# A mixture-of-experts stage on one TensorE: weights stationary and tokens streaming in the gate and up products

## The reference, cut to what matters

```python
    # top-1 of 4 groups, top-2 of 8 experts in it: 2 slots per token, sorted by expert,
    # each expert's slots padded to blocks of MOE_BLOCK = 128
    xs = h_pad[slot_tok].reshape(n_blocks, MOE_BLOCK, d)

    def expert_block(args):
        xb, e = args
        return (jax.nn.silu(xb @ exp_w_gate[e]) * (xb @ exp_w_up[e])) @ exp_w_down[e]

    yb = lax.map(expert_block, (xs, blk_e)).reshape(n_slots, d)
```

## Time and profile before

| | |
|---|---|
| median of 3 runs | 8363.2 us (8362.91 to 8382.72) |
| the profiled execution | 8377.1 us, span 8375.4 us |
| mean granted TensorE clock | 0.877 |
| PE busy | 6258.6 us (75%) |
| PEld busy | 4170.1 us (50%) |
| DVE busy | 4465.4 us (53%) |
| ACT busy | 3932.8 us (47%) |
| POOL busy | 1101.7 us (13%) |
| DMA | 751.33 MB, mean 90 GB/s |

### The profile page before, as it was taken

The page is one execution under the profiler, slowest core; times in us unless marked ns, Lnnn a source line. Parts: engine busy times, 40 slices in busy tenths (PEclk is TensorE's granted clock), DMA queues, the critical chain, the costliest instruction groups (busy, mean ns, idle before and its releaser), DMA issues. The chain is left out here.

```text
span 8375.4 us, 113418 instructions
## 1 busy us (share of the span) xinstructions
PE 6258.6 (75%) x38615; PEld 4170.1 (50%) x38615; DVE 4465.4 (53%) x10927; ACT 3932.8 (47%) x7814; POOL 1101.7 (13%) x1560
## 2 busy tenths in 40 slices
PE   6999976888777877888888771632299969999950
PEld 2777752555455555555555450621155546677630
DVE  0221227878778778888877749246255631010025
ACT  0212215788777878888888750123232312222124
POOL 1222210000000000000000000022022223333333
PEclk8999988999999999999999985765588879999975
DMA  5211210000000000000000001225432238888877
GB/s 191 63 59 59 61 55 3 8 11 11 10 11 11 11 11 11 10 9 10 10 11 9 6 23 45 101 72 61 64 96 94 90 131 327 325 336 335 321 270 246
DMA packets 315242, 751.33 MB, mean 90 GB/s; under 512 B 110701, under 2 KB 174189, under 8 KB 272568
## 3 DMA queue, kind: packets, MB, share of 16 engines
q0 software_dynamic: 70400, 424.79, 13.8%
q1 hardware_dynamic: 244388, 321.14, 13.0%
q10 hardware_dynamic: 54, 0.30, 0.0%
HBM read 582.03 MB, written 162.11 MB: 89 GB/s over the span
## 5 line engine op out<-in xcount | busy, mean ns | idle before, releaser
L955 PE MATMUL at_pC<-at_mark,at_identb 128*128 128x256 bf16 (+1 forms) x5708 | 756.7, 283 | 385.9 <-DVE at_mark L1090 303.8
L1012 DVE CUSTOM_DVE_ANT_0 at_sm<-at_pS,at_drop 128x512 f32<-128x512 f32 (+3 forms) x1152 | 696.1, 642 | 321.1 <-PE at_pS L911 319.1
L955 PEld LDWEIGHTS at_pC<-at_mark,at_identb 128*128 128x128 bf16 x5708 | 531.3, 101 | 638.8 <-DVE at_mark L1090 463.8
L846 ACT ACTIVATE at_sm<-at_sm,at_negm 128x512 f32<-128x512 f32 (+3 forms) x1152 | 785.6, 695 | 58.7 <-DVE at_negm L1017 58.3
L911 PE MATMUL at_pS<-keep_KT,at_q 64*128 64x512 f32 (+3 forms) x2304 | 648.1, 641 | 204.8 <-DVE at_mx L1012 204.5
L1004 DVE SCALAR_TENSOR_TENSOR at_score<-at_relu,keep_IW,at_score 128x512 f32<-128x512 f32 (+3 forms) x994 | 660.2, 706 | 120.5 <-ACT at_relu L831 116.9
L901 PE MATMUL at_pD<-keep_IKT,at_iq_stack 128*128 128x512 bf16 (+3 forms) x2272 | 579.5, 377 | 147.6 <-ACT at_relu L831 97.5
L932 PEld LDWEIGHTS at_pO<-at_pt_sb,keep_V 128*64 128x64 f32 x8448 | 470.6, 141 | 416.4 <-issue 291.1
L831 ACT ACTIVATE at_relu<-at_pD 128x512 f32<-128x512 f32 (+3 forms) x1136 | 580.7, 568 | 105.9 <-PE at_pD L901 66.5
L921 PE MATMUL at_pT<-keep_ident,at_sm 128*128 128x128 f32 x4224 | 588.6, 282 | 40.6 <-DVE at_out L1026 32.5
L932 PE MATMUL at_pO<-at_pt_sb,keep_V 128*64 128x128 f32 x8448 | 613.3, 288 | 0.1
(11 more groups left out here) (442 smaller groups left out, 10892.3 us busy)
## 6 DMA issues: line engine op xcount, KB each, us to landing
scratch_ys<-ex_y SPq DMA_DIRECT2D x96, 512.0 KB, 2.6
ada_w_sb<-in_ada_w SPq DMA_DIRECT2D x12, 2048.0 KB, 8.0
scratch_x<-mx_x SPq DMA_DIRECT2D x33, 512.0 KB, 7.5
scratch_h<-mx_h SPq DMA_DIRECT2D x33, 512.0 KB, 2.6
cb_x<-scratch_x SPq DMA_DIRECT2D x33, 512.0 KB, 4.4
pj_x<-in_x_prompt SPq DMA_DIRECT2D x32, 512.0 KB, 3.6
mx_x<-in_x_prompt SPq DMA_DIRECT2D x32, 512.0 KB
out_y_prompt<-cb_out SPq DMA_DIRECT2D x32, 512.0 KB, 3.6
```

What stands on the lines that cost most here:

```text
L846: last = e.activation(row, row, ACT.Exp, bias=negm[:, x.group % 16, kv:kv + 1], scale=-1.0, accum_out=den[:, x.side, kv * G + x.g, x.c:x.c ...
L955: last = e.matmul(pC[:, side, 0:b - a], identb[:, :], mark[:, a:b], start=a == at.start, stop=not constant and b == at.stop)
L1012: last = e.tensor_tensor_reduce(sm[:, u % RING, kv, 0:x.width], pS[:, kv, 0:x.width], drop[:, o:o + x.width], -HD ** -0.5, -NEG, ALU.add, ...
```

## The change

Gate and up products change sides: a block of 128 x 128 of the weights is stationary and the 128 tokens of xT stream past it. The results then come out with the inner width on the partitions, in two pieces of 128 columns, and g is at once what the down products take. The transposes of g, the tile pH, VectorE's copy and the semaphores g and gT go; hT gets two buffers; VectorE's second product is written to hT, after a wait for the down products of two blocks before; TensorE's gate product waits for hT of the block before in place of g.

```diff
-        sg = sb("ex_sg", [P, FE]); gu = sb("ex_gu", [P, FE]); g = sb("ex_g", [P, FE]); hT = sb("ex_hT", [P, FC, P]); y = sb("ex_y", [P, 2, D])
-        pT = pb("ex_pT", [P, DC, P]); pg = pb("ex_pg", [P, CUT]); pu = pb("ex_pu", [P, CUT]); pH = pb("ex_pH", [P, FC, P]); pY = pb("ex_pY", [P, 2, CUT])
+        sg = sb("ex_sg", [P, FE]); gu = sb("ex_gu", [P, FE]); hT = sb("ex_hT", [P, 2, FC, P]); y = sb("ex_y", [P, 2, D])
+        pT = pb("ex_pT", [P, DC, P]); pg = pb("ex_pg", [P, CUT]); pu = pb("ex_pu", [P, CUT]); pY = pb("ex_pY", [P, 2, CUT])
...
                         pair(e, "w", b, par, 2)
-                        wait(e, s["g"], b)
+                        wait(e, s["hT"], b)
                         for dst, src in ((pg, wg), (pu, wu)):
-                            for c in range(DC):
-                                last = e.matmul(dst[:, 0:FE], xT[:, par, c, :], src[:, par, c * FE:(c + 1) * FE], start=c == 0, stop=c == DC - 1)
+                            for f in range(FC):
+                                for c in range(DC):
+                                    block = src[:, par, c * FE:(c + 1) * FE].rearrange("p (f c) -> p c f", c=FC)[:, f, :]
+                                    last = e.matmul(dst[:, f * P:(f + 1) * P], block, xT[:, par, c, :], start=c == 0, stop=c == DC - 1)
                         last.then_inc(s["gu"], 1)
...
-                                last = e.matmul(pY[:, k, :], hT[:, c, :], wd[:, q, c * D + k * CUT:c * D + (k + 1) * CUT], start=c == 0, stop=c == FC - 1)
+                                last = e.matmul(pY[:, k, :], hT[:, q, c, :], wd[:, q, c * D + k * CUT:c * D + (k + 1) * CUT], start=c == 0, stop=c == FC - 1)
                             last.then_inc(s["down"], 1)
-                    b = st
-                    if valid(b):
-                        e.wait_ge(s["g"], b + 1)
-                        wait(e, s["hT"], b)
-                        gv = g[:, :].rearrange("p (f c) -> p c f", c=FC)
-                        for c in range(FC):
-                            last = e.transpose(pH[:, c, :], gv[:, c, :], ident)
-                        last.then_inc(s["gT"], 1)
...
-                        wait(e, s["gT"], b)
                         e.tensor_tensor(gu[:, :], pg[:, 0:FE], sg[:, :], ALU.mult).then_inc(s["gsig"], 1)
                         e.wait_ge(s["gsig"], b + 1)
-                        e.tensor_tensor(g[:, :], pu[:, 0:FE], gu[:, :], ALU.mult).then_inc(s["g"], 1)
-                        e.wait_ge(s["gT"], b + 1)
-                        wait(e, s["down"], 2 * b)
-                        e.tensor_copy(hT[:, :, :], pH[:, :, :]).then_inc(s["hT"], 1)
+                        wait(e, s["down"], 2 * (b - 1))
+                        e.tensor_tensor(hT[:, par, :, :].rearrange("p c n -> p (c n)"), pu[:, 0:FE], gu[:, :], ALU.mult).then_inc(s["hT"], 1)
+                        e.wait_ge(s["hT"], b + 1)
```

## The result

| | before | after |
|---|---|---|
| median | 8389.2 us (15 runs, 8362.9 to 8394.6) | 8405.7 us (15 runs, 8390.4 to 8418.3) |
| ratio | | 1.0025, 95% interval 1.0016 to 1.0033 |
| the profiled execution | 8377.1 us, clock 0.877 | 8390.4 us, clock 0.879 |

The change costs 0.25%: +21 us, between +13 and +28 (the two medians lie 16.5 us apart, which is within that). Forecast was +6 with -1 to +14. With more runs than stood ahead of the prediction the median of before is 8389, so absolute times say less than the ratio. One thing is to be known about the profile of after: it shows the fastest of its 15 executions (8390.4; the clock averaged over all 15 is 0.877, not 0.879).

The account below looks back on a forecast made before the run. The weights' loop through POOL and DMA was taken to bound most steps: 0.23 us growth x 0.31 is 0.07, times 96 +7 us, ends -0.95, together +6 on 8363.2, giving 8369 us; range 8348 to 8400.

Parts of the forecast that it names:

- the size of a pass: Gate and up in the experts: 64 passes over 128 columns at 111.7 ns each, 7.15 us, growing by 0.23 us.
- the upper bound of 0.31: Largest growth in us of gate and up per step, at 113 ns per pass as in the transposes of x.
- The base of the absolute time: Median of the runs before, 8363.2 us, to which the forecast added +6 us to give 8369 us.
- less 1 for the end: Last down products no longer wait for the transposes of g and the copy: -0.95 us, once.
- The share of 0.31: Part of a growth in the weights' loop through POOL and DMA that reaches the step period, a/(1+a).
- a slope of -0.45: Line through 64 steps: a wd issued 1 us later moves the weights two steps on by only 0.45 us.
- The slot of the transposes and VectorE's copy: Removed 0.22 us of TensorE and 0.42 us of VectorE per step, outside the loop; TensorE's counts only in 17 steps without wait.
- the rival of a held POOL: VectorE's copy of hT delays POOL's wd; removal gains up to 12 us, about 8350; chance 0.11, shared with fewer clock drops.
- The first rival: Longer waits ahead of the gate product make TensorE's clock drop more often: +34 us to about +80; chance 0.10.
- Loads that are not hidden: Rival: gate and up's 0.19 us weight loads surface under 108 ns streams; +190 to about +390 us; chance 0.04.
- the serial case: Gate and up's loads fully serial: 64 x 0.19 is 12.2 us, step 16.8 us, about +390 us, 8760.
- Same: Outcome that whole-kernel time stays within 25 us (0.3%), what a measurement can tell; chance 0.78.

Follow-up runs that it names:

- e2_proj_stride2: Kernel before with the projection's stationary blocks at line 496 taken as every second column of 256, not 128 contiguous ones; 128 passes take 15.09 us, time 8411 us.
- e3_keep_slot: Changed kernel, but TensorE still does two transposes of hT, into a tile nobody reads, behind the down products; ratio 1.0020 to before.
- the filled pair: Kernel before and changed kernel, each with three useless products (0.67 us) ahead of each wait for gate weights; ratios 0.9979 and 1.0018 to before.
- e4: Kernel before without the transposes of g and VectorE's copy, second product written untransposed to hT, gate and up products unchanged; ratio 1.0008 to before.
- e1: Changed kernel with gate and up's stationary blocks as 128 contiguous columns instead of every second column; ratio 1.0024 to before.
- e11: Kernel before with wd fetched one step later, behind the next block's wg and wu, with its own index tile; 8276.4 us, ratio 0.9852 to before.

## Why the prediction was wrong, point by point

**The step that failed is the size of a pass.** The prediction took 111.7 ns from line 496 "for it is the same operation", and from the transposes of x that a stride adds next to nothing. It is not the same operation: with every second column as the stationary side it takes 117.8 ns, in the experts and in the projection alike. Gate and up grew by 0.63 us, not by 0.23, twice the upper bound of 0.31. The transposes of x, with a stride of eight, do run at some 112 ns, and why that stride costs them next to nothing was not found. That they are transposes is not the reason, for the trace of before holds the very stride of two as well, in the transposes of g (line 2233), whose loads the prediction did not use:

```profile
L2233 PEld LDWEIGHTS ex_pH<-keep_ident,ex_g x192: 194/196/222, 6862.7 to 8074.1; 128*128 128x128 f32 x192
```

Their median is the 196 ns of e2_proj_stride2, where the earlier trace rows have 193 for the stride of eight. And the second transpose of g starts 118 ns ahead of the first of x, on the average, against 109 in e3_keep_slot, whose two transposes take contiguous columns of hT. A neighbouring row bounded the price of one difference through another stride, and that was no bound.

**The base of the absolute time.** Of the 42.5 us between the 8363.2 that the forecast started from and the 8405.7 measured, 26 are the base: two of the three executions that it had were the two fastest of the fifteen. On 8389.2 the forecast's +6 would have been 8395. This is bad luck and a range too narrow for three runs; it says nothing of the mechanism, while the +0.25% against the forecast's +0.07% does.

**The working behind it fits, but its share is not shown.** With the measured 0.63 the prediction's own formula gives 0.63 x 0.31 x 96 = 19 us, less 1 for the end: +18, inside the measured +13 to +28. This is one sum against one number. The share of 0.31 comes from a slope of -0.45, and that depends on which steps are kept: by the gate starts of the same stretch it is -0.46 for the 65 steps that have a wait under 1.9 us and no slow gate in them or next, -0.11 with those next to a slow gate, and -0.26 if waits under 0.3 us are left out instead. The share that reaches the period should be more than 0.31 in the steps that have no wait, where TensorE's own work counts in full (+0.41 us); the filled pair, with most steps of that kind, fits: 33 us, of 39 possible.

**The slot of the transposes and VectorE's copy: right.** Outside the loop, worth nothing on balance (e3, e4). In e4 the wd gather starts 11.42 us after the gate, as with the copy, so the rival of a held POOL falls; in after it is 12.05 us, later by the 0.63 us, where 11.65 was forecast.

**The clock: the mechanism was seen, its direction was not.** The first rival said that the change lengthens waits and so brings clock drops, and by 0.06 us only. In fact TensorE's work grew by 0.41 us per step and the profiled run of after has fewer slow gates (3, though over all runs its mean clock equals that of before). What the prediction lacked is that more waiting and more slow gates come with shorter work as well. Two cases fit: e1 (0.39 us less for the passes, no gain seen, mean clock 0.8756 where before has 0.8767 on that chip) and e4 (0.22 us less work outside the loop, no gain, 0.8757). That the clock paid e1's gain back is argued from these numbers and not shown by a run of its own.

**Loads that are not hidden: wrong as priced, and yet on the right side.** They stay hidden at full size: the stride costs 6 ns per pass, not the 48 or more of that rival. Its price for the serial case was itself too low: 64 x 0.19 counts the loads alone, and with the 0.108 us of each stream behind them gate and up would take 19.1 us. The Trainium skill (TensorE: Matmul & The Clock Gate, LDWEIGHTS) gives a load's time by its number of columns alone. In these traces the load's record grows from 192 to 196 ns with a stride of two at the same 128 columns, and the pass by 6 ns. The Trainium skill's ratio for a sustained stream at 128 columns (the same page, Back-to-back issue gap) would have given 156 ns, by the prediction's estimate. None of these runs bears that out: 111.6 to 117.9.

**The chances.** "Same" held the measured +0.25% within its bound of 0.3%; the time of 8405.7 lies above the range, which ended at 8400. The change itself, +13 to +28 us, lies at or above the upper end of the sum's -1 to +14.

## What to carry to other kernels

Before pricing a matmul by another line of the trace, compare the access pattern of the stationary side as well as shape and type: in f32 at full clock, every second column cost 6 ns on each 128-column pass, and here turning the roles round made 64 passes per step pay it where none of the 32 did before. Look for any row of the trace with the same stride, of whatever operation, before taking one with another stride. Where TensorE waits 1 to 2 us per step on a transfer, look for the loop that issues the transfer; shortening TensorE's step gave nothing measurable here, while moving one gather (and giving it its own index tile) gave 1.5%, after which the same 0.4 us of TensorE work counted in full. When a gather is moved to later, list what must wait for its landing, the index tile that it reads included.

## What the runs showed of the hardware that was not expected

- A stride of two elements in an f32 stationary block: 117.8 ns per pass in place of 111.6, at 128 columns and full clock, with the DMA's share at 0.26 and at 0.87 alike, and 196 ns for a load's record in place of 192. A stride of eight in transposes: about 112 ns and 193.
- Useless matmuls in a wait made the kernel before 18 us faster (0.9979, interval 0.9970 to 0.9989), with the mean granted clock up from 0.877 to 0.879: 0.67 us of them per step, outside the loop. Behind some of the waits of 1.9 to 5.0 us the gate product ran in part at 1.2 GHz and took mostly 1.7 us longer, 5.41 against 3.72 us; behind others of 2.0 to 3.0 us it did not. In before, after, e1 and e4 the next step then had no wait, and the one after it waited 1.4 us or more again, wherever this happened in the steady part.
- The 16 DMA engines moved 366 GB/s at a busy share of 0.99 while TensorE was busy all the time, with 4.2 MB per step of 11.47 us (e11); TensorE's passes over 256 columns took 216 ns, as in the earlier trace rows.
